# Input weights of a transformer trunk kernel in two parts, with the query, key and value columns ahead of the pool columns

## What is computed

```python
h = rms_norm(x, norm1_g)
proj = einsum('bsd,de->bse', h, w_in)          # 1280 columns: u 512 | q 512 | k 128 | v 128
a = pool_mixer(u, pool_w, pool_scale)          # trailing window means of 2, 4, 8, 16 frames minus u, then a map
b = swa_sink_attention(q, k, v, ...)           # 8 query heads, 2 key/value heads, window of 128 frames
x = x + einsum('bse,ed->bsd', concatenate([a, b]), w_out)
hid = square(relu(einsum('bsd,df->bsf', rms_norm(x, norm2_g), w_up)))
x = x + einsum('bsf,fd->bsd', hid, w_down)
```

## Time and profile before

| | |
|---|---|
| median of the runs | 875.68 us |
| span of the profiled execution, first to last instruction | 873.5 us |
| PE busy | 864.2 us, 99% |
| DVE busy / ACT busy / POOL busy | 530.7 / 418.7 / 270.5 us |
| chain of work that ended last | PE 89%, DVE 5%, DMA 3%, ACT 2%, POOL 1% |
| DMA over the span | mean 147 GB/s |

### The profile page before, as it was taken

One profiled execution on the slowest core, in us unless ns is written; L12 is line 12 of the kernel. 1 busy time (PEld: TensorE's weight loads), 2 busy tenths in 40 slices (PEclk: granted clock), 3 DMA queues, 4 the chain that ended last, 5 costly groups with the idle time before them and its releaser, 6 DMA issues.

```text
span 873.5 us, 10960 instructions
## 1 busy us (share of the span) xinstructions
PE 864.2 (99%) x4128; PEld 715.6 (82%) x4128; DVE 530.7 (61%) x800; ACT 418.7 (48%) x746; POOL 270.5 (31%) x202
## 2 busy tenths in 40 slices
PE   8999999999999999999999999999999999999998
PEld 6888888788888788888888888888888888888886
DVE  7666558944458576666666656466845464646462
ACT  7566658632246655556555555444333333333330
POOL 0633445300231243222333222004544004444440
PEclk9999999999999999999999999999999999999999
DMA  8311221551111465444455542889752553242422
GB/s 349 122 49 49 96 99 49 170 188 78 49 48 44 163 201 171 134 134 133 156 181 159 167 133 85 299 317 390 246 191 97 169 193 120 94 148 95 146 97 73
DMA packets 66341, 128.38 MB, mean 147 GB/s; under 512 B 3569, under 2 KB 19953, under 8 KB 66289
## 3 DMA queue, kind: packets, MB, share of 16 engines
q1 hardware_dynamic: 66144, 127.68, 42.4%
q10 hardware_dynamic: 144, 0.01, 0.0%
HBM read 89.92 MB, written 37.75 MB: 146 GB/s over the span
## 4 chain that ended last, share of the span: by engine, by line
PE 89%; DVE 5%; DMA 3%; ACT 2%; POOL 1%; issue 0%; SPq 0%; ACTq 0%; DVEq 0%; POOLq 0%
PE bank L1244 28%; PE bank L1245 28%; PE bank L1246 28%; DMA mem<-in_w_in 1%; PE bank L1359 1%; PE bank L1257 1%; DVE t_M L1033 1%; PE bank L1344 1%; DVE ring L1025 1%; PE bank L1374 1%; POOL mem L497 1%; DMA raw<-in_w_up 1%; PE bank L1334 1%; DMA h_keep<-h_buf 1%; DVE wgt L924 0%
## 5 line engine op out<-in xcount | busy, mean ns | idle before, releaser
L1244 PE MATMUL bank<-b_op,s_op 128*128 128x512 f32 x448 | 174.4, 389 | 0.0
L1246 PE MATMUL bank<-b_op,s_op 128*128 128x512 f32 x448 | 174.3, 389 | 0.0
L1245 PE MATMUL bank<-b_op,s_op 128*128 128x512 f32 x448 | 174.3, 389 | 0.0
L564 POOL TENSOR_TENSOR b_sum<-d_raw,d_raw 128x1024 f32<-128x1024 f32 x40 | 97.7, 2442 | 200.4 <-DVE b_op L1068 200.4
L1064 DVE TENSOR_TENSOR s_op<-s_in,s_op 128x1024 fp32r<-128x1024 f32 x56 | 74.3, 1327 | 125.1 <-ACT s_op L767 124.9
L767 ACT ACTIVATE s_op<-s_in 128x1024 fp32r<-128x1024 f32 x56 | 59.4, 1060 | 177.4 <-PE bank L1246 147.1
L1244 PE MATMUL bank<-wgt,xs 128*128 128x256 f32 (+1 forms) x320 | 121.0, 378 | 1.7 <-DVE wgt L918 1.4
L1245 PE MATMUL bank<-wgt,xs 128*128 128x256 f32 (+1 forms) x320 | 118.4, 370 | 0.0
L1246 PE MATMUL bank<-wgt,xs 128*128 128x256 f32 (+1 forms) x320 | 118.1, 369 | 0.0
L1025 DVE TENSOR_TENSOR ring<-raw,ring 128x512 fp32r<-128x512 f32 x96 | 88.2, 933 | 30.7 <-ACT ring L715 29.5
L1244 PE MATMUL bank<-xs,ring 128*128 128x512 f32 x256 | 99.9, 390 | 1.3 <-DVE h_buf L1047 1.2
(11 more groups left out here) (125 smaller groups left out, 1356.0 us busy)
## 6 DMA issues: line engine op xcount, KB each, us to landing
s_in<-h_keep SPq DMA_DIRECT2D x56, 512.0 KB, 3.7
h_keep<-h_buf SPq DMA_DIRECT2D x16, 1280.0 KB, 5.1
raw<-in_w_up SPq DMA_DIRECT2D x16, 1024.0 KB, 6.5
d_raw<-in_w_down SPq DMA_DIRECT2D x32, 512.0 KB, 7.6
mem<-in_x SPq DMA_DIRECT2D x16, 512.0 KB, 4.6
h_keep<-h_buf SPq DMA_DIRECT2D x16, 512.0 KB, 3.9
mem<-in_w_in SPq DMA_DIRECT2D x8, 640.0 KB, 8.0
mem<-in_x_T SPq DMA_DIRECT2D x8, 512.0 KB, 3.8
```

The lines of the kernel that those rows point to most:

```text
L564: nc.gpsimd.tensor_tensor(out=b_sum[G % 2], in0=group_rows(qa, g), in1=group_rows(qb, g), op=op).then_inc(b_summed, 1)
L1244: nc.tensor.matmul(out_ap, lhs[HI], rhs[HI], start=first, stop=False, skip_group_check=chained)
L1245: nc.tensor.matmul(out_ap, lhs[HI], rhs[LO], start=False, stop=False, skip_group_check=chained)
L1246: return nc.tensor.matmul(out_ap, lhs[LO], rhs[HI], start=False, stop=last, skip_group_check=chained)
```

## The change

The weights are held as two areas, one of 768 columns (q, k, v) per block and one of 512 (u). SP first loads the eight q/k/v blocks, with `x_T` of tile 1 after the third, then `x` of tile 0, then the eight u blocks, five of them without a wait; `x_T` of tile 0 is issued by ACT, ahead of the small `columns` tensor. ACT and DVE split in that order. PE makes the q/k/v blocks of tiles 0 and 1 in turn, tile 1 into banks 5, 6, then all u blocks of tile 0, then those of tile 1 with `transpose_in(0)` in their middle. From tile 2 on all q/k/v blocks come first, then `transpose_in(t-1)`, then all u blocks. `x_high(1)` leaves ACT's round loop; `sum_squares_x(1)` stays behind `copy_u(0)`. `score(0)` waits for tile 1's copies, whose banks it takes. The semaphores of one group of the MLP's loads are merged into those of another.

```diff
-    KV_B, Q_B, U_B = 2, 3, 4
+    KV_B, Q_B, U_B = [2, 5] + [2] * (NT - 2), [3, 6] + [3] * (NT - 2), [4, 2] + [4] * (NT - 2)
...
-            load_xT(0)
-            for k in range(6):
-                load_w_in(k)
+            for k in range(3):
+                load_w_qkv(k)
+            load_xT(1)
+            for k in range(3, KT):
+                load_w_qkv(k)
             load_x(0)
-            load_w_in(6)
-            load_w_in(7)
-            load_xT(1)
+            sp.wait_ge(setup_dve, 1 + 2 * PAIRS)
+            for k in range(KT):
+                load_w_u(k)
...
             def split_w_out(k):
-                sc.wait_ge(in_done, KT * (NT - 1) + (2 * D * (k + 1) - 1) // (2 * IN_W) + 1)
+                end = 2 * D * (k + 1)
+                blocks = (min(end, W_U_AT) - 1) // (2 * QKV_W) + 1
+                if blocks < KT:
+                    sc.wait_ge(qkv_step, blocks)
+                else:
+                    sc.wait_ge(q_done, NT)
+                if end > W_U_AT:
+                    sc.wait_ge(in_done, KT * (NT - 1) + (end - W_U_AT - 1) // (2 * POOL_W) + 1)
...
+            sc.dma_start(xT_slot[0], x_T[0]).then_inc(xT_in[0], 16)
             sc.dma_start(cols, columns).then_inc(cols_in, 16)
             x_high(0, (0,))
             sc.wait_ge(cols_in, 16)
-            split_w_in(0, (0, 1, 2))
-            split_w_in(1, (0, 1))
-            split_w_in(2, (0,))
+            split_w_qkv(0)
+            split_w_qkv(1)
             x_high(0, (1,))
-            for k in range(3, KT):
-                split_w_in(k, (0,))
+            split_w_qkv(2)
+            x_high(1, (0,))
+            split_w_qkv(3)
+            split_w_qkv(4)
+            x_high(1, (1,))
+            for k in range(5, KT):
+                split_w_qkv(k)
             sum_squares_x(0)
+            for k in range(KT):
+                split_w_u(k)
             for t in range(NT):
-                if t + 1 < NT:
+                if 1 <= t < NT - 1:
                     x_high(t + 1)
                 if 1 <= t < NT - 1:
                     sum_squares_x(t + 1)
...
-            for t in range(NT):
-
-                b = {1: 4, NT - 1: 4}.get(t, 5)
-                project_in(t, range(0, b))
-                if t >= 1:
+            for t, k in [(0, 0), (0, 1), (0, 2), (1, 0), (0, 3), (1, 1), (0, 4), (1, 2), (0, 5), (1, 3),
+                         (0, 6), (1, 4), (0, 7), (1, 5), (1, 6), (1, 7)]:
+                project_qkv(t, (k,))
+            project_u(0, range(KT))
+            for t in range(1, NT):
+                if t >= 2:
+                    project_qkv(t, range(KT))
                     transpose_in(t - 1)
-                project_in(t, range(b, KT))
+                    project_u(t, range(KT))
+                else:
+                    project_u(t, range(KT // 2))
+                    transpose_in(t - 1)
+                    project_u(t, range(KT // 2, KT))
                 if t >= 2:
                     transpose_probs(t - 2)
-                if t >= 1:
-                    mix(t - 1)
-                    score(t - 1)
+                mix(t - 1)
+                score(t - 1)
                 if t >= 2:
                     attend(t - 2)
```

More of the change, by code:

```diff
@@ L223, in hybrid_trunk, with qkv_pieces, qkv_count @@
         dn_group, dn_done, dn_evac = sem("dn_group"), sem("dn_done"), sem("dn_evac")
[L225 to L234, removed]
+        KV_COLS, Q_COLS, QKV_COLS = slice(Q_W, QKV_W), slice(0, Q_W), slice(0, QKV_W)
+        def qkv_pieces(k):
+            return (KV_COLS, Q_COLS) if k == 0 else (QKV_COLS,)
+        def qkv_count(k, cols):
+            return 1 + k + (1 if k or cols == Q_COLS else 0)
         NTOK = 2 * NT
@@ L647, in copy_u @@
                 sc.wait_ge(in_done, KT * (t + 1))
-                nc.scalar.activation(u_tok, bank[U_B][:, :], ACT.Copy, scale=rinv[:, t:t + 1]).then_inc(u_copied, 1)
+                nc.scalar.activation(u_tok, bank[U_B[t]][:, :], ACT.Copy, scale=rinv[:, t:t + 1]).then_inc(u_copied, 1)
             def evac_u(t):
@@ L1267, in project_in @@
                     if t == 0:
-                        pe.wait_ge(w_in_lo, w_count(k, KV_COLS))
+                        pe.wait_ge(w_qkv_lo, qkv_count(k, KV_COLS))
                     first, stop = k == 0, k == KT - 1
-                    if k == 0 and t >= 1:
-                        pe.wait_ge(kv_copied, t)
-                    last = passes(bank[KV_B][:, 0:KV_W], lhs(k), rhs(k, POOL_W + Q_W, KV_W), first, stop)
+                    if k == 0 and t >= 2:
+                        pe.wait_ge(kv_copied, 1 if t == 2 else t)
+                        if t == 2:
+                            pe.wait_ge(u_copied, 2)
+                    last = passes(bank[KV_B[t]][:, 0:KV_W], x_parts(t, k), rhs(k, KV_COLS), first, stop)
                     if stop:
@@ L1275, in project_in, with project_u @@
                     if t == 0:
-                        pe.wait_ge(w_in_lo, w_count(k, Q_COLS))
-                    elif k == 0:
-                        pe.wait_ge(q_copied, t)
-                    last = passes(bank[Q_B][:, :], lhs(k), rhs(k, POOL_W, Q_W), first, stop)
+                        pe.wait_ge(w_qkv_lo, qkv_count(k, Q_COLS))
+                    if k == 0 and t >= 2:
+                        pe.wait_ge(q_copied, 1 if t == 2 else t)
+                    last = passes(bank[Q_B[t]][:, :], x_parts(t, k), rhs(k, Q_COLS), first, stop)
                     if stop:
                         last.then_inc(q_done, 1)
+                    elif t == NT - 1:
+                        last.then_inc(qkv_step, 1)
+            def project_u(t, ks):
+                for k in ks:
                     if t == 0:
-                        pe.wait_ge(w_in_lo, w_count(k, U_COLS))
-                    elif k == 0:
-                        pe.wait_ge(u_copied, t)
-                    last = passes(bank[U_B][:, :], lhs(k), rhs(k, 0, POOL_W), first, stop)
+                        pe.wait_ge(w_u_lo, k + 1)
+                    if k == 0 and t == 1:
+                        pe.wait_ge(kv_copied, 1)
+                    if k == 0 and t >= 2:
+                        pe.wait_ge(u_copied, 1 if t == 2 else t)
+                    last = passes(bank[U_B[t]][:, :], x_parts(t, k), [w_u_s[:, k, part, :] for part in (HI, LO)],
+                                  k == 0, k == KT - 1)
                     last.then_inc(in_done, 1)
```

103 lines of the change are left out of this document (64 added, 39 removed).

## The result

The changed kernel takes 884.52 us (884.02 to 885.25, 4 runs), the kernel before beside it 875.63 (875.42 to 875.72, 4 runs): ratio 1.0103, 95% interval 1.0092 to 1.0115, so 8.9 us slower. The forecast was 884.9. The profiled execution has a span of 882.0 us (before 873.5) and a time of 884.13.

What follows compares the result with a forecast made beforehand. PE, busy 99% of the span, was taken as the bound. Span 873.5 - 0.5 (start) + 7.0 (`mix(0)`) + 2.1 (clock) + 0.6 (last round) = 882.7; the median, 2.2 higher, 884.9 us, range 881.2 to 887.0.

Steps and rivals of the forecast that it cites:

- Start, -0.5: Tiles 0 and 1 up to the end of their q/k/v blocks: 0.5 us gained, between -2.0 and +0.5.
- The point chosen between the ends, 6.55: ACT's first weight split: expected at 6.55 us, between 5.65 (all hidden) and 7.0 (frames slowed, columns after them).
- The rival that the alternation buys nothing: Start: worse, tiles 0 and 1 in turn buy nothing, transfers set the pace; inside the start's range, no own chance.
- `mix(0)`, +7.0: PE waits at `mix(0)` for tile 2's late load, the chain behind it and POOL's squares: +7.0 us, +5.8 to +7.4.
- The rest that the prediction put at 2.6: Wait at `mix(0)` even without the load: transposes to result 6.3 us, PE arrives after 3.7, so 2.6 us.
- Clock, +2.1: PE's clock falls in the `mix(0)` stall, work behind it starts at half rate: +2.1 us, between 0 and 2.5.
- The rival with the clock kept, 882.8: Same stall at `mix(0)`, but PE's full rate goes on behind it: 882.8 us, chance 0.16.
- Rounds 2 to 6, 0: Transposes to `mix` 7.4 us, result needs 7.2: just hidden, 0, up to +1 us over five rounds.
- Last round, +0.6: PE waits 0.5 us for tile 6's result, next wait on DVE 0.6 later: +0.6 us, between 0 and +1.9.
- The sum: All terms added to the profiled span before: 873.5 - 0.5 + 7.0 + 2.1 + 0.6 = 882.7 us; median 884.9.
- Not slower, 875.3 to 877.7: Rival: tile 2's load does not hold `mix(0)`, wait 2.6 us, clock stays: 875.3 to 877.7 us, chance 0.06.

Runs made afterwards that it cites:

- frames_on_sp: Changed kernel with tile 0's frames issued first on SP's queue, ahead of the weights, `columns` alone on ACT's: 883.41 us, ratio 1.0091.
- in_order: Changed kernel with all q/k/v blocks of tile 0 made before those of tile 1, without alternation: 885.02 us, ratio 1.0114.
- squares_first: Changed kernel with tile 1's square sum ahead of `copy_u(0)`, so tile 2's frames load sooner: 881.55 us, ratio 1.0068.
- squares_and_hold: squares_first plus a wait holding POOL's head squares of tiles 1 and 7 behind DVE's subtraction: 879.95 us, ratio 1.0051.
- filler: Changed kernel with 54 unread transposes of the identity on PE ahead of `mix(0)`: 883.21 us, ratio 1.0089.
- round_one: Changed kernel with `transpose_in(0)` after two u blocks of tile 1, square sums of tiles 1 and 2 ahead of `copy_u(0)`, POOL's squares held: 878.19 us, ratio 1.0032.
- relaid: Changed kernel with tile 0's frames first on SP, earlier square sum, POOL's squares held, transposes before all tile 1 u blocks, further reordering: 875.96 us, ratio 1.0006.
- fill_mix: squares_and_hold with the first four q/k/v blocks of tile 2 made ahead of `mix(0)`: 880.82 us, ratio 1.0063.
- last_round: Changed kernel with tile 6's transposes after the fifth q/k/v block of tile 7 instead of the eighth: 884.42 us, ratio 1.0102.
- warm_longer: Changed kernel with 36 transposes of the identity at PE's start instead of 24: 884.62 us, ratio 1.0104.
- columns_first: Changed kernel with the small `columns` tensor issued ahead of tile 0's frames on ACT's queue: 885.26 us, ratio 1.0113.
- relaid_pool: relaid with POOL's inverse roots (tile 2's, tile 1's heads) moved behind tile 0's window sums: 875.84 us, ratio 1.0003.

## Why the prediction was right

**Start, -0.5.** 7.87 for 7.8, 12.36 for 12.2, and PE at `mix(0)` 0.57 us sooner. The point chosen between the ends, 6.55 for ACT's first split, was 6.62. Of the parts, the frames on ACT's queue with `columns` behind them cost 1.1 us (frames_on_sp); the alternation is worth 0.5 us in the medians, within their scatter (in_order). The rival that the alternation buys nothing is not excluded.

**`mix(0)`, +7.0.** Idle 6.45 us, and 44.53 - 37.92 = 6.6 from PE's arrival. The mechanism, the late load of tile 2's frames and its square sums in front of `evac_u(0)`, is shown by squares_first: 3.1 us of stall and 3.0 of median go with it. The rest that the prediction put at 2.6 without the load and without the squares was 2.76 in squares_and_hold. The squares were mis-sized: L966 took 1.39 for 0.43 as argued, but removing them gave 0.6 at `mix(0)`, for 1.2. The Trainium skill ("SBUF — State Buffer", "Terms") calls the port pair of DVE and GpSimd an exclusive lock, where the loser "fully blocks": the trace agrees, POOL's squares at 42.00 hold DVE's additions from 42.15, and they end at 43.54, 0.29 behind the squares' end.

**Clock, +2.1.** Measured +1.93 (4.00 - 2.07 us), and 1.8 by filler. That the fall would come is shown; how near the size came is in part luck of the profile, since the same stall cost 1.7 to 2.8 us in the others, the last beyond the 2.5 that the prediction took as its upper end. The rival with the clock kept, 882.8, is out for this stall; for a stall of 1.38 us (round_one) the clock was kept.

**Rounds 2 to 6, 0.** Tile 2 starts 48.53 - 40.56 = 7.97 us late, and no wait is added until `mix(6)`.

**Last round, +0.6.** `mix(7)` is at 176.50 for 167.88, 8.62 late, so +0.65. The size is right, its working only in part: `mix(6)` waits 1.23, not 0.5, since POOL's squares of tile 7 fell on DVE's subtraction (1.96 us for 0.90), and the wait at tile 7's transposes, expected 0.6 later, is gone. Two errors cancel here. squares_and_hold shows the pair: 0.18 at the one place, 0.61 at the other.

**The sum.** -0.57 + 6.6 + 1.93 + 0.65 = 8.6 us; the spans differ by 8.5.

**Not slower, 875.3 to 877.7.** Its condition, `evac_u(0)` within 1 us of the transposes, was not met (34.17 to 37.71), and the prediction named the right point to look at. Its price was wrong (and its terms add up to 877.8 at the upper end). squares_first meets the condition (0.7 us) and takes 881.55: the wait is then 3.37 us and not 2.6, and the clock does not stay. Without the squares too, the wait is 2.76, the clock falls again, and it is 879.95. relaid meets it as well (`evac_u(0)` at 31.21, the transposes at 30.52) and takes 875.96, but with more of PE's work behind the transposes and a better start, which this rival did not have.

## What to carry to other kernels

When a stage is reordered, follow each in-order queue from the moved result to the next consumer and list what now stands in front of it: here one square sum that waits for a load cost 3 us because it came ahead of a copy out of a bank, and filling PE's stall with other work moved the stall one round on. Time the new distance between producer and consumer on PE against the chain beside it (here 3.7 us against 6.3), and price a long stall of PE with the slower matmuls behind it (every one of 2.76 us and more cost 1.5 to 2.8 us here, those of 1.38 at `mix(0)` and 2.42 at `mix(1)` nothing). A single profile gives one draw of that price, so compare the time without it. Put the transfer that the first operation needs first on the queue that carries the others.

## What the runs showed of the hardware that was not expected

**The clock after a stall.** It stayed at 1.00 across an idle 1.38 us (round_one) and an idle 2.42 us (fill_mix, at `mix(1)`, every window from 56 to 66 us), had fallen after 2.76 us (squares_and_hold), and after 3.37 us it fell only once work had resumed, 1.4 to 3.4 us into it (squares_first: 1.00 in 42 to 44, 0.57 in 44 to 46). Of the profiles with a stall of some 6.4 us, last_round's has fallen by 40.5 us, warm_longer's not before 43, though PE ran out of work at about the same time in both (37.7 and 37.9). So the fall is not tied to the moment of the stall, and the cost can lie behind matmuls that ran at full rate.

**Half rate in a start without long stalls.** The changed kernel's windows show 1.00 throughout its start. With nearly the same start, squares_first had 0.69 and 0.74 at 9 to 12 and 12 to 15 us, filler 0.51, fill_mix 0.56 and round_one 0.52 at 9 to 12, in_order 0.84 and 0.59 at 6 to 9 and 9 to 12, columns_first 0.76 and 0.67 at 9 to 12 and 12 to 15. It cost 0.6 to 1.15 us by tile 1's last block. It goes with the idle time ahead of the first useful matmul. The five profiles with a gap of 1.59 to 1.87 us (round_one, filler, columns_first, in_order, fill_mix) all have it; of the four with 0.87 to 1.04 us (squares_and_hold, the changed kernel, last_round, squares_first) only the last has it; warm_longer, frames_on_sp, relaid and relaid_pool, with 0.5 us or less, have not, nor has the kernel before with 1.03. That the gap is the cause is argued, not shown. It is also not all of the scatter: relaid_pool scatters by 1.5 us with a mean granted clock of 1.00 in all of its 11 runs.

**Two queues at the start.** The same 512 KB were there at 4.47 us as the first transfer on the queue of the weights, at 5.36 on another queue beside them, and at 6.76 there behind a small one.
